# Key selection of six prompt tiles inside the projection stage of a hybrid decoder step

## The reference, cut to what matters

```python
D_MODEL, SEQ, C_CONV, CONV_W = 1024, 2048, 512, 31
N_HEADS, N_KV_HEADS, HEAD_DIM, N_IDX_HEADS, IDX_DIM = 8, 4, 64, 8, 64
TOPK_MAX, Q_BLOCK = 256, 128

def project_inputs(x, w_in, b_in):
    h = jnp.einsum('bsd,dn->bsn', x, w_in) + b_in
    ca, cb, q, k, v, qi, ki, wi, gates = jnp.split(h, list(SPLIT_POINTS), axis=-1)
    u = ca * jax.nn.sigmoid(cb)
    ...

def indexer_select(qi, wi, kidx, qpos, k_sel):
    dots = jnp.einsum('bqhd,bsd->bqhs', qi, kidx) * (IDX_DIM ** -0.5)
    score = jnp.einsum('bqhs,bqh->bqs', jax.nn.relu(dots), wi).astype(jnp.float32)
    kpos = jnp.arange(kidx.shape[1])
    score = jnp.where(kpos[None, None, :] <= qpos[None, :, None], score, -jnp.inf)
    return lax.top_k(score, k_sel)[1]

def block(i):                       # dsa_prompt, 16 tiles of 128 queries
    idx = indexer_select(sl(qi), sl(wi), ki, qpos, k_sel)
    valid = idx <= qpos[None, :, None]
    return sparse_attend(sl(q), gather_rows(k, idx), gather_rows(v, idx), valid)
```

## Time and profile before

| | us |
|---|---|
| median of 3 runs | 3293.84 (3284.55 to 3295.58) |
| the profiled execution | 3294.07 |
| its span, first to last instruction | 3292.3 |
| TensorE busy in it | 2881.6 (88%) |
| VectorE, ScalarE, GpSimd busy | 1913.2, 1124.2, 902.1 |

### The profile page before, as it was taken

One profiled execution on the slowest core, in us unless ns is written; L12 is line 12 of the kernel. 1 busy time (PEld: TensorE's weight loads), 2 busy tenths in 40 slices (PEclk: granted clock), 3 DMA queues, 4 the chain that ended last, 5 costly groups with the idle time before them and its releaser, 6 DMA issues. The chain is left out here.

```text
span 3292.3 us, 45511 instructions
## 1 busy us (share of the span) xinstructions
PE 2881.6 (88%) x14961; PEld 1791.1 (54%) x14962; DVE 1913.2 (58%) x2848; ACT 1124.2 (34%) x1870; POOL 902.1 (27%) x1292
## 2 busy tenths in 40 slices
PE   8999999999956777788986767899996899999988
PEld 7887799999922334454554544444443333333333
DVE  1699312998257888888777635464435343434337
ACT  2111221111355858595867745300100111111112
POOL 3344333333233523232324531014120100000013
PEclk9999999999967888898998989999997899999989
DMA  3323232335210110110110057445332777768347
GB/s 129 101 91 99 84 115 68 99 119 160 90 54 13 39 48 29 49 36 26 59 33 13 15 184 283 147 147 185 128 121 106 253 278 292 273 253 304 136 152 237
DMA packets 237860, 415.44 MB, mean 126 GB/s; under 512 B 29108, under 2 KB 156340, under 8 KB 224890
## 3 DMA queue, kind: packets, MB, share of 16 engines
q1 hardware_dynamic: 180514, 272.79, 24.6%
q0 software_dynamic: 25216, 89.03, 8.0%
q10 hardware_dynamic: 31968, 51.49, 4.3%
HBM read 518.08 MB, written 96.91 MB: 187 GB/s over the span
## 5 line engine op out<-in xcount | busy, mean ns | idle before, releaser
L387 PE MATMUL p_ps_acc<-p_x_hi,p_w_hi 128*128 128x352 f32 (+2 forms) x1480 | 525.6, 355 | 7.7 <-POOL p_w_lo L319 6.0
L387 PE MATMUL p_ps_acc<-p_x_lo,p_w_hi 128*128 128x352 f32 (+2 forms) x1480 | 523.2, 354 | 0.0
L387 PE MATMUL p_ps_acc<-p_x_hi,p_w_lo 128*128 128x352 f32 (+2 forms) x1480 | 522.9, 353 | 0.0
L633 DVE SCALAR_TENSOR_TENSOR g_shared<-p_uh,p_taps,g_shared 128x1024 f32<-128x1024 f32 x240 | 388.5, 1619 | 8.5
L2754 PE MATMUL e_ps_G<-l_wgu,e_xT 128*64 x768 | 342.0, 598 | 22.3 <-DVE g_shared L2871 10.4
L2756 PE MATMUL e_ps_G<-g_shared,e_xT 128*64 128x512 f32 x768 | 342.2, 599 | 0.0
L387 PEld LDWEIGHTS p_ps_acc<-p_x_hi,p_w_hi 128*128 128x128 f32 (+1 forms) x1480 | 277.1, 187 | 37.9 <-POOL p_w_lo L319 6.7
L387 PEld LDWEIGHTS p_ps_acc<-p_x_lo,p_w_hi 128*128 128x128 f32 (+1 forms) x1480 | 278.5, 188 | 28.8 <-issue 0.5
L387 PEld LDWEIGHTS p_ps_acc<-p_x_hi,p_w_lo 128*128 128x128 f32 (+1 forms) x1480 | 277.2, 187 | 27.1
L1244 DVE TENSOR_SCALAR_CACHE_REDUCE q_junk_dve<-q_sc,q_mid 128x640 bf16<-128x640 f32 (+6 forms) x175 | 247.0, 1411 | 77.4 <-POOL q_mid L1359 75.0
L1023 PE MATMUL q_ps_s<-a_keys,q_q_st 64*128 64x512 f32 (+3 forms) x640 | 165.1, 629 | 114.1 <-DVE q_top L1292 92.5
(11 more groups left out here) (454 smaller groups left out, 4887.0 us busy)
## 6 DMA issues: line engine op xcount, KB each, us to landing
l_wgu<-in_w_gate_dram SPq DMA_DIRECT2D x96, 1024.0 KB
l_wgu<-in_w_up_dram SPq DMA_DIRECT2D x96, 1024.0 KB
l_wd<-in_w_down_dram SPq DMA_DIRECT2D x96, 1024.0 KB
p_w<-in_w_in_dram SPq DMA_DIRECT2D x72, 512.0 KB
yb<-e_y SPq DMA_DIRECT2D x48, 512.0 KB
featT<-p_stage ACTq DMA_DIRECT2D x28, 528.0 KB
featT<-p_stage ACTq DMA_DIRECT2D x28, 512.0 KB
x_gates<-featT SPq DMA_DIRECT2D x48, 256.0 KB
```

The costliest lines, as they stand in the source:

```text
L387: m = nc.tensor.matmul(acc[slot][tb][0:rows, 0:width], wp[:, slot, k, 0:rows], xp[:, k, at], start=(k == 0 and i == 0), stop=(k == KD - 1 ...
L633: ch.mark(nc.vector.scalar_tensor_tensor(dst, src, wt, dst, ALU.mult, ALU.add))
```

## The change

The index dots, the sums, the search and the choice of tiles 2 to 7 are moved into the second half of `front`. Attention finds their masks ready, in a buffer `early` of its own. In `front`:

- Dots: 40 steps of up to 512 keys (EARLY_STEPS), two per chunk from block NS + 3 to NS + 9, one in the middle of a `product` and one behind it. ScalarE's relu and VectorE's sums stand beside `evict` and `gated`. They pass through the two banks `kv` and `kw`, one step at a time: TensorE's step i waits for relu i - 1.
- Search: 50 rounds, each for three tiles, counted on ScalarE (three operations per round, reading `early`), with GpSimd's step `narrow` of five operations behind it. Blocks NS + 11 to NS + 30 have 3 and 2 rounds in turn. GpSimd's loop does the rounds of block n - 1 behind the split of block n.
- Choice: VectorE does it between the steps of the layer norm, with two more full-length operations per tile than attention has, since it makes the mask too.
- SyncE loads the second half of the keys after that choice, as they share the memory.

In attention the other eight tiles are searched in pairs (SEEK). The pairs 14, 15 and 8, 9 are searched in 8 slots each, the pairs 12, 13 and 10, 11 in 16 slots each. The table TILES puts tiles 6, 7 and 4, 5 and 2, 3 under dots, and the branches lie in slots 0 to 15, 24 to 31 and 40 to 47. No dots stand ahead of slot 0.

```diff
+EARLY_AT = NS + 3
+SEARCH_AT = NS + 11
+EARLY_TILES = [2, 3, 4, 5, 6, 7]
+EARLY_GROUPS = [(7, 4, 2), (6, 5, 3)]
+EARLY_COL = {t: 3 * g + i for g, tiles in enumerate(EARLY_GROUPS) for i, t in enumerate(tiles)}
+EARLY_ROW = {t: P * sum(i + 1 for i in EARLY_TILES if i < t) for t in EARLY_TILES}
+EARLY_STEPS = [(t, m, a, min(a + 512, (t + 1) * P)) for t in EARLY_TILES for m in range(4) for a in range(0, (t + 1) * P, 512)]
...
+def early_points():
+    at = 0
+    for n in range(EARLY_AT, NS + 9 + 1):
+        for tb in range(3):
+            for h in range(2):
+                if at < len(EARLY_STEPS):
+                    yield (n, tb, h), at
+                    at += 1
...
+def early_rounds():
+    p = 0
+    for n in range(SEARCH_AT, 2 * NS):
+        for tb in range(3 if (n - SEARCH_AT) % 2 == 0 else 2):
+            if p < 2 * HALVINGS:
+                yield (n, tb), p
+                p += 1
...
@@ front, sync @@
+                sp.wait_ge(e_chosen, 1)
+                until(sp, NS + KI_BLK + 1)
+                sp.dma_start(kT[:, :, T // 2:T], c.featT[COL_K:COL_V, T // 2:T].rearrange("(b p) t -> p b t", p=P)).then_inc(k_loaded, 16)
+                sp.wait_ge(k_loaded, 16)
...
@@ front, gpsimd @@
+                def begin():
+                    pool.wait_ge(e_ready, 1)
+                    pool.wait_ge(u_turned, 1)
+                    for r in range(HALVINGS):
+                        ch.mark(nc.gpsimd.memset(e_pow2[:, r], 0.5 ** (r + 1)))
+                    for t in EARLY_TILES:
+                        ch.mark(nc.gpsimd.memset(e_bound[:, EARLY_COL[t]:EARLY_COL[t] + 1], (t + 1) * P - 2 * 256 + 0.5))
+                    ch.mark(nc.gpsimd.tensor_copy(e_least, e_lowest))
+                    ch.link(nc.gpsimd.tensor_tensor(e_span, e_most, e_lowest, ALU.subtract))
+                    ch.link(nc.gpsimd.tensor_tensor(e_width, e_pow2.to_broadcast([P, HALVINGS, 6]),
+                                                    e_span.rearrange("p (r t) -> p r t", r=1).to_broadcast([P, HALVINGS, 6]), ALU.mult))
+                    ch.link(nc.gpsimd.tensor_scalar(e_width, e_width, 1.0, 1e-30, ALU.mult, ALU.add))
+                    nc.gpsimd.tensor_tensor(e_mid[:, 0], e_least, e_width[:, 0], ALU.add).then_inc(e_mids, 1)
+                def narrow(p):
+                    r, at = p // 2, slice(3 * (p % 2), 3 * (p % 2) + 3)
+                    if r == HALVINGS - 1:
+                        return
+                    if p < 2:
+                        pool.wait_ge(e_mids, 1)
+                    ch.mark(nc.gpsimd.tensor_tensor(e_mid[:, r + 1, at], e_mid[:, r, at], e_width[:, r + 1, at], ALU.subtract))
+                    for i, t in enumerate(EARLY_GROUPS[p % 2]):
+                        col = slice(EARLY_COL[t], EARLY_COL[t] + 1)
+                        pool.wait_ge(e_counted, 3 * p + i + 1)
+                        ch.mark(nc.gpsimd.tensor_scalar(e_step[:, col], e_count[:, r, col], (t + 1) * P - 2 * 256 + 0.5, e_width[:, r, col], ALU.is_le, ALU.mult))
+                    ch.sync()
+                    nc.gpsimd.tensor_tensor(e_mid[:, r + 1, at], e_mid[:, r + 1, at], e_step[:, at], ALU.add).then_inc(e_mids, 1)
+                    pool.wait_ge(e_mids, p + 2)
...
+                    if n == SEARCH_AT:
+                        begin()
+                    for tb in range(3):
+                        if (n - 1, tb) in early_round_at:
+                            narrow(early_round_at[n - 1, tb])
...
@@ front, tensor @@
+                def early_dots(i):
+                    t, m, a, b = EARLY_STEPS[i]
+                    if i == 0:
+                        pe.wait_ge(ki_loaded, 32)
+                        pe.wait_ge(e_weighed, 1)
+                    else:
+                        pe.wait_ge(e_kept, i)
+                    for x in range(2):
+                        rows = slice(x * HD, x * HD + HD)
+                        nc.tensor.matmul(both[:, x, 0:b - a], e_qi[rows, m, (t - 2) * P:(t - 1) * P], kiT[rows, a:b], start=True, stop=True).then_inc(e_full, 1)
...
+                        if (n, tb, 0) in EARLY_POINTS:
+                            product(n, tb, [0, 1, 2, 3])
+                            early_dots(EARLY_POINTS[n, tb, 0])
+                            product(n, tb, [4, 5, 6, 7])
+                        else:
+                            product(n, tb, list(range(KD)))
+                        if (n, tb, 1) in EARLY_POINTS:
+                            early_dots(EARLY_POINTS[n, tb, 1])
...
@@ front, scalar @@
+                def early_relu(i):
+                    t, m, a, b = EARLY_STEPS[i]
+                    act.wait_ge(e_full, 2 * i + 2)
+                    if i >= 2:
+                        act.wait_ge(e_used, i - 1)
+                    nc.scalar.activation(e_relu[i % 2][:, :, 0:b - a], both[:, :, 0:b - a], ACT.Relu, scale=float(HD) ** -0.5).then_inc(e_kept, 1)
+                def early_count(p):
+                    r, g = p // 2, p % 2
+                    act.wait_ge(e_mids, max(1, p))
+                    for k, t in enumerate(EARLY_GROUPS[g]):
+                        i = EARLY_COL[t]
+                        if 3 * p + k >= 2:
+                            act.wait_ge(e_counted, 3 * p + k - 1)
+                        nc.scalar.activation((e_sure, e_edge)[(p + k) % 2][:, 0:(t + 1) * P], early_row(early, t), ACT.Sign, bias=e_mid[:, r, i:i + 1], scale=-1.0,
+                                             accum_out=e_count[:, r, i:i + 1]).then_inc(e_counted, 1)
...
+                        if (n, tb, 0) in EARLY_POINTS:
+                            early_relu(EARLY_POINTS[n, tb, 0])
                         evict(n, tb)
+                        if (n, tb, 1) in EARLY_POINTS:
+                            early_relu(EARLY_POINTS[n, tb, 1])
+                        if (n, tb) in early_round_at:
+                            early_count(early_round_at[n, tb])
...
@@ front, vector @@
+                def early_sum(i):
+                    t, m, a, b = EARLY_STEPS[i]
+                    row = early_row(early, t)[:, a:b]
+                    if i == 0:
+                        dve.wait_ge(e_weighed, 1)
+                        dve.wait_ge(tri_made, 2)
+                    dve.wait_ge(e_kept, i + 1)
+                    for x in range(2):
+                        src, wt = e_relu[i % 2][:, x, 0:b - a], wi_tok[:, t, 2 * m + x:2 * m + x + 1]
+                        if m == 0 and x == 0:
+                            ch.link(nc.vector.tensor_scalar(row, src, wt, None, ALU.mult))
+                        elif x == 0:
+                            ch.link(nc.vector.scalar_tensor_tensor(row, src, wt, row, ALU.mult, ALU.add))
+                        else:
+                            nc.vector.scalar_tensor_tensor(row, src, wt, row, ALU.mult, ALU.add).then_inc(e_used, 1)
+                            dve.wait_ge(e_used, i + 1)
...
+                def early_bounds():
+                    dve.wait_ge(e_counted, 6 * HALVINGS)
+                    dve.wait_ge(e_mids, 2 * HALVINGS - 1)
...
+                    ch.link(nc.vector.tensor_tensor(e_low, e_low, e_least, ALU.max))
+                def early_choice(t):
+                    n, at = (t + 1) * P, slice(EARLY_COL[t], EARLY_COL[t] + 1)
+                    row = early_row(early, t)
+                    select_row_tile(ch, nc, row, e_low[:, at], e_high[:, at], e_need[:, at], e_sure[:, 0:n], e_edge[:, 0:n], row)
...
                         gated(half, b)
+                        until_gated = EARLY_POINTS[NS + 2 * b + 3, 2, 1] if half and 0 <= b < CB - 1 else 0
+                        while done < until_gated:
+                            early_sum(done)
+                            done += 1
...
                         for q in (2, 3, 4):
                             sum_of(q)
+                        early_bounds()
+                        early_choice(7)
                         centre(2)
+                        early_choice(6)
                         sum_squares(2)
                         centre(3)
                         keep_variance(2)
+                        early_choice(5)
                         sum_squares(3)
                         diagonals(2)
                         centre(4)
                         keep_variance(3)
                         rescale(2)
+                        early_choice(4)
+                        early_choice(3)
+                        early_choice(2)
+                        dve.sem_inc(e_chosen, 1)
                         sum_squares(4)
...
@@ attend_prompt @@
-HUGE = 2.0 ** 100
-HALVINGS = 25
 NSLOT = 4 * NT
-SC_SLOTS = 6
-SEARCHED = list(range(2, NT))
-TILES = [0, 1, 4, 5, 10, 11, 14, 15, 12, 13, 8, 9, 6, 7, 2, 3]
+SC_SLOTS = 4
+TILES = [0, 1, 6, 7, 14, 15, 4, 5, 12, 13, 2, 3, 10, 11, 8, 9]
+SEEK = [14, 15, 12, 13, 10, 11, 8, 9]
+DOTS_FROM = [0, 8, 24, 40]
+SEEK_FROM, SEEK_SLOTS = [8, 16, 32, 48], [8, 16, 16, 8]
+def seek_length(j):
+    return (SEEK[j] + 1) * P
...
-PER_SLOT = 5
```

(27 more changed lines are left out.)

336 lines of the change are left out of this document (197 added, 139 removed).

## The result

The changed kernel takes **3210.4 us** (median of 4, 3202.0 to 3213.7) against 3289.2 us for the kernel before on the same chip: a ratio of **0.976, 95% interval 0.974 to 0.978**. On another chip it came out at 0.974 (0.973 to 0.976). The prediction was 3301 with a range of 3235 to 3360: it forecast a small loss, and the change gains 79 us, more than any of its cases. In the profiled executions the span falls from 3292.3 to 3199.6 us, by 92.7.

The account below looks back on a forecast made before the run. TensorE was taken to bound the projection's second half, no engine attention. +30 +10 +57 +9 = +106 in the projection against -99 in attention: +7 on 3294.07, so 3301 us, range 3235 to 3360.

Parts of the forecast that it names:

- The windows of attention: Attention's eight windows of eight slots: with selection work taken out they fall from 980 to 906 us, -74.
- Counts stay in the chain: Attention, slots 16 to 23: search counts remain in the serial chain, so the window was put at 126 us.
- attention shrinks more: Rival on attention's windows: a line through them gives 832, corrected about 870, not 906; time 3265; chance 0.13.
- The search rounds: Projection beside the convolution: GpSimd's rounds at 4.8 us each make blocks 16.1 us and hold up TensorE, +57.
- the bounds (2 and 7.4): Price of a search round: 2 us if no operation meets a tap, 7.4 if all five wait for one.
- GpSimd slips between the taps: Rival on the search rounds: a round costs 2 to 3.5 us, the term 0 to 20, time 3254; chance 0.22.
- The keys' second half is hidden: Projection's end: the 1 MB load comes some 18 us before the stage's end and costs nothing.
- Dots and sums: Projection's second half: early dots add +30 to a full TensorE, and late VectorE sums that meet splits add +10.
- The tail: Layer norm at the projection's end: three choices on VectorE make TensorE wait 7.6 us and restart at lower clock, +9.
- The lead-in: Start of attention: only query load, one score and one maximum remain, some 8 us of 33.5, -25.
- The clock rival: Rival: TensorE's clock falls in the projection's gaps, 10 to 30 us more, time 3320; chance 0.07.
- `begin`'s fills: Projection, start of the search: GpSimd's single-column fills take 1 us, +0; about +35 if each waited for a tap.

Follow-up runs that it names:

- n3: Changed kernel with the searches of tiles 12, 13 and 10, 11 at full rate (8 slots) in place of half rate (16 slots): 3249.8 us, ratio 0.988.
- n2: Kernel before, in its old order, with the selection of tiles 2 to 7 left out of attention: 3153.3 us, ratio 0.958.
- n1: Changed kernel without any early work in the projection, the masks of tiles 2 to 7 a buffer of zeros: 3129.2 us, ratio 0.950.
- n8: Kernel before with only the load of the keys' second half moved to SyncE's queue at the stage's end: ratio 0.999.
- n12: Kernel before with tensor `uh` allocated ahead of `x_hi` and `x_lo`, so these lie higher in SBUF: single execution, last product ends at 899.7.
- n11: Kernel before with PSUM banks `kv` and `kw` allocated as one tensor of two banks: single execution, last product ends at 904.5.
- n14: Changed kernel with the choices of tiles 3 and 2 moved on VectorE, and three search rounds in every block until all 50 are done: ratio 0.977.
- n9: Changed kernel with 5 of the 25 rounds of the early search, dots, sums and choices kept: ratio 0.970.
- n4: Changed kernel with four more idle GpSimd subtractions in each early search round, nine operations in place of five: 3260.8 us, ratio 0.991.
- n5: As n4, but each of the four extra subtractions waits for the end of the one before: ratio 0.993.
- n6: Changed kernel with each search round's first subtraction issued directly behind the last addition of the round before, without a wait: ratio 0.979.

## Why the prediction was wrong, step by step

The forecast was +7 on the profiled execution, the outcome -93. The 100 us between them:

- **The windows of attention, 61 us too long.** This is the largest term and the step that failed: the ratio of a window to its fullest engine. I took 1.17 and 1.21 from rows of before in which the search runs at full rate, and applied them to windows at half rate, for which no row stood. Full rate does give 1.29 and 1.26 there (n3), half rate 1.13 and 1.12. These two windows are 37 of the 61 us. The second factor hangs on the first: I took 103 us of TensorE work for the third window from a row at clock 0.93, and it is 94 at 0.98, in a window with shorter waits. "Counts stay in the chain" holds at full rate, 147 us for the 126 that I gave, and not at half rate. Of the other 24 us, 13 are in slots 48 to 55 and 5 to 7 each in the first, second and fourth window, where I took rows less work, and the last window is 5 longer than forecast; no run takes these apart. The rival *attention shrinks more* had the right sign and 870 us. The same stretch takes 845, nearer to the 832 of its uncorrected line through the windows; I gave the case 0.13. In the old order too the removal alone gives more than I had allowed for everything (110 against 74, n2).
- **The search rounds, +24 and not +57.** The mechanism was the right one: GpSimd's small operations wait for taps, the next split stands behind them, TensorE waits for the split and for nothing of ScalarE's. The term that was mis-sized is the price of a round, 3.4 us for 4.8; the bounds (2 and 7.4) held. I also left out the gaps between GpSimd's operations, 1.2 us a block. So GpSimd needed 13.9 us a block and not 16.1, where TensorE alone takes 12.6 for the same 16 blocks (n1) and not 12.1. That is 16 x 1.3 = 21 of the 24 us. Averaging 2.5 rounds over the blocks was no error that these runs show. The rival *GpSimd slips between the taps*, 2 to 3.5 us a round, is what happened, with its 20 us at the upper end; it had 0.22.
- **The base, 12 us that I had at nothing.** "The keys' second half is hidden" looked at where the load goes and not at what it leaves: in its old place it held up the weights, 4.4 us of waiting (n8). And the operands moved in SBUF, which makes every product 0.6% faster, 5 us by the last one (n12 beside n11); nothing in the trace of before could tell that. The remaining 3 are within what traces of the same stage differ by.
- **Dots and sums, 45 for 40.** 40 steps at 1.13 us where I had 0.75 for the step itself, from the two steps of the earlier trace rows, and 0.25 for waits on VectorE's sums. TensorE is busy throughout and no such wait shows, so the steps were 15 us too cheap and the waits of 10 weren't there. That the sum came out near is luck.
- **The tail, 13 for 9.** The wait was where it was forecast and 11.2 us long for 7.6. The three choices took 17.3 us for 15.2, since two of their operations met GpSimd's split of 939 to 943. The restart at a lower clock was there too (0.94 over the last 116 us).
- **The lead-in, -24 for -25**, and later stages 4 us shorter. These same stages, untouched, take 1339 to 1372 us in the 15 experiments, so 4 us of them say nothing.
- **The clock rival** has its place: in the search stretch TensorE's work is 230.5 us at clock 0.98 against 224.3 at 1.00 without early work, 6 of the 24 us. With more waits it grows: n14 has 237.6 at 0.95.

**`begin`'s fills cost GpSimd nothing**, as the Trainium skill, "SBUF — State Buffer", section "Who interferes with whom", has it for instructions that only write. The trace agrees for the fills: they take the 0.89 us of the earlier trace rows, as without VectorE. But VectorE's operation beside them was the first tap, which has one input in SBUF and not the two of which the Trainium skill speaks there, so the case with two isn't seen here. And that tap did not go free:

```profile
614.79 0.89 POOL L373 MEMSET p_unew<- 128x1 f32 x25
...
614.32 2.10 DVE L795 TENSOR_SCALAR g_shared<-p_uh,p_taps,g_cols 128x1024 f32<-128x1024 f32 x1
```

It took 1.29 us in the earlier trace rows and 1.27 in n1, also with the end of a split beside it but without fills, and 1.45 in n9, which has 20 fills fewer. So VectorE lost 0.8 us beside the fills; the time of the kernel doesn't show it.

The two large errors have one source. Both terms were prices per unit, one for a window and one for a round, taken from rows in which the engines meet more tightly than where they were used. For the window n3 shows it; for the round it is my reading: in the earlier trace rows VectorE's long operations follow one another, and between two taps there is a small one. I saw that the two terms of 100 us stood against each other and gave both signs about even chances, 0.40 faster and 0.45 slower; but the range ended at 3235 since I didn't let the two low cases come true together. They did: 3301 - 61 - 33 is 3207. With the 12 us of the base it is 3195, 15 from the measured time.

## What to carry to other kernels

Work that is taken out of a stage that no engine fills returns more than the ratio of window to fullest engine says, when what it leaves is spread thinner: halving the rate of a serial search was worth 34 us here with no work removed. A background chain costs what it exceeds the foreground's block by, with the gaps between its operations counted in: 2.3 rounds a block cost 0.8 us a block here, and each round above that 3 to 4. Once the foreground that it collides with is over, the rest is cheap, so the cost saturates. And when two favourable rivals rest on the same bias in the rows, put the range's end where both hold.

## What was not expected of the hardware

- The same stream of products takes 160.0 or 159.0 ns from one to the next (11.52 and 11.45 us for 72) depending on where its operands lie in SBUF, with clock 1.00 in both. In n12 the last product ended 5 us earlier than in n11 on the same chip.
- A small GpSimd operation beside VectorE's 1.29 us taps takes 0.57 to 0.75 us on average, 0.2 to 0.3 alone; between two taps, around a 0.25 us operation, three of them passed in 0.5 us. Averaged over a round it is 0.62 to 0.77 us an operation, for five or nine in a round and with or without waits between (the changed kernel, n4, n5, n6).
- A VectorE operation of two SBUF inputs that meets a split was stretched from 1.29 to 3.4 us, as in the earlier trace rows. One with a single SBUF input took 2.10 us for 1.29 beside 31 GpSimd fills of one column.
- A 1 MB load in the middle of the stage delayed the weights behind it by some 3 us, though DMA was busy to only 0.39 of its time in that stretch.
